# Start of a two-block transformer kernel: raw x transposed by columns, inverse root applied at the first projection's evictions

## The reference

```python
h = rms_norm(x, norm_g[layer])            # x * rsqrt(mean(x*x) + 1e-6) * norm_g
proj = jnp.einsum('bsd,de->bse', h, w_in[layer])   # w_in: 2048 x 8192
qa, ka, va, ga, qb, kb, vb, gb = jnp.split(proj, splits, axis=-1)   # eight of 1024 columns
```

## Time and profile before

| | us |
|---|---|
| three runs: median (lowest to highest) | 1999.19 (1998.39 to 2001.27) |
| the profiled execution, its own time | 2001.09 |
| its span, first to last instruction | 1999.4 |
| TensorE busy | 1921.9 (96% of the span) |
| DVE busy | 1360.1 (68%) |
| ACT busy | 1050.0 (53%) |

### The profile page before, as it was taken

One profiled execution on the slowest core, in us unless ns is written; L12 is line 12 of the kernel. 1 busy time (PEld: TensorE's weight loads), 2 busy tenths in 40 slices (PEclk: granted clock), 3 DMA queues, 4 the chain that ended last, 5 costly groups with the idle time before them and its releaser, 6 DMA issues.

```text
span 1999.4 us, 30270 instructions
## 1 busy us (share of the span) xinstructions
PE 1921.9 (96%) x9674; PEld 1603.0 (80%) x9674; DVE 1360.1 (68%) x1838; ACT 1050.0 (53%) x1687; POOL 104.6 (5%) x181
## 2 busy tenths in 40 slices
PE   7999999999999999999889998999999999999998
PEld 5887887778787777777678777888888888888886
DVE  5677775667777745556777776777777776655555
ACT  5544545554445454446664444556656665544444
POOL 1000001101000013320000000000000000000000
PEclk9999999999999999999999998999999999999999
DMA  7788776578788854336557976577777766555554
GB/s 255 268 292 263 244 260 219 178 244 302 259 290 285 287 167 116 112 125 213 187 194 261 316 248 219 184 244 231 241 230 242 231 220 189 178 186 192 190 192 144
DMA packets 236729, 444.80 MB, mean 222 GB/s; under 512 B 14190, under 2 KB 110027, under 8 KB 235259
## 3 DMA queue, kind: packets, MB, share of 16 engines
q1 hardware_dynamic: 235242, 434.39, 66.0%
q0 software_dynamic: 1424, 9.63, 1.2%
HBM read 439.72 MB, written 4.24 MB: 222 GB/s over the span
## 4 chain that ended last, share of the span: by engine, by line
PE 83%; DVE 6%; ACT 4%; DMA 3%; issue 3%; SPq 1%; DVEq 0%; ACTq 0%
PE PS L1659 51%; PE PS L1969 16%; PE PS L1970 8%; DMA ada_raw<-in_w_ada 3%; PE PS L1690 1%; ACT w_hi L621 1%; DVE arena L1075 1%; PE PS L1748 1%; PE PS L1751 1%; DVE w_lo L1025 1%; PE PS L1734 1%; PE PS L1759 1%; DVE s_sb L1190 1%; PE PS L1688 1%; DVE smx L1198 0%
## 5 line engine op out<-in xcount | busy, mean ns | idle before, releaser
L1025 DVE TENSOR_TENSOR w_lo<-raw,w_hi 128x1024 fp32r<-128x1024 f32 x618 | 755.4, 1224 | 490.3 <-ACT w_hi L621 483.2
L1659 PE MATMUL PS<-w_hi,aT 128*128 128x512 f32 (+1 forms) x3264 | 1049.0, 395 | 16.8 <-ACT arena L757 7.8
L621 ACT ACTIVATE w_hi<-raw 128x1024 fp32r<-128x1024 f32 x618 | 653.6, 1059 | 654.1 <-PE PS L1659 431.9
L1659 PEld LDWEIGHTS PS<-w_hi,aT 128*128 128x128 f32 x3264 | 614.5, 189 | 158.4 <-issue 12.5
L1659 PE MATMUL PS<-w_lo,aT 128*128 128x512 f32 (+1 forms) x1632 | 635.3, 389 | 0.0
L1969 PE MATMUL PS<-aT,w_hi 128*128 128x512 f32 x1408 | 489.3, 394 | 0.3 <-DVE aT L1154 0.3
L1970 PE MATMUL PS<-aT,w_lo 128*128 128x256 f32 x1408 | 390.2, 277 | 0.0
L1659 PEld LDWEIGHTS PS<-w_lo,aT 128*128 128x128 f32 x1632 | 308.6, 189 | 58.8 <-issue 0.2
L1969 PEld LDWEIGHTS PS<-aT,w_hi 128*128 128x128 f32 x1408 | 264.0, 188 | 61.9 <-DVE aT L1154 0.5
L1075 DVE SCALAR_TENSOR_TENSOR arena<-ada_raw,silu_c,arena 128x1024 f32<-128x1024 f32 x192 | 246.5, 1284 | 42.2 <-DMA ada_raw<-in_w_ada 42.1
L1970 PEld LDWEIGHTS PS<-aT,w_lo 128*128 128x128 f32 x1408 | 264.3, 188 | 0.2 <-issue 0.2
(11 more groups left out here) (212 smaller groups left out, 1268.4 us busy)
## 6 DMA issues: line engine op xcount, KB each, us to landing
raw<-in_w_in SPq DMA_DIRECT2D x256, 512.0 KB, 4.1
ada_raw<-in_w_ada SPq DMA_DIRECT2D x192, 512.0 KB, 4.9
raw<-in_w_up SPq DMA_DIRECT2D x176, 512.0 KB, 3.5
raw<-in_w_down SPq DMA_DIRECT2D x88, 512.0 KB, 3.9
raw<-in_w_out SPq DMA_DIRECT2D x32, 512.0 KB, 5.3
raw<-in_w_o SPq DMA_DIRECT2D x32, 512.0 KB, 5.2
raw<-in_w_uq SPq DMA_DIRECT2D x18, 512.0 KB, 5.2
raw<-in_w_ukv SPq DMA_DIRECT2D x16, 512.0 KB, 4.2
```

What stands on the lines that cost most here:

```text
L621: nc.scalar.activation(w_hi[:, m % RING, :], raw[:, m % RING, :], ACT.Copy).then_inc(hi_ready, 1)
L1025: nc.vector.tensor_tensor(w_lo[:, m % RING, :], raw[:, m % RING, :], w_hi[:, m % RING, :].bitcast(F32), ALU.subtract).then_inc(lo_ready, 1)
L1659: mm = pe.matmul(dst, l, r, start=first and j == 0, stop=last and j == 2)
```

## The change

The row factor moves from x to the results, and the start is ordered by what each step needs.

- SP: x comes in three column pieces, 256, 768 and 1024 columns of both tiles, each with its own semaphore and each followed by a weight chunk; chunk 3 follows. The parameters (12 DMAs) come behind the weights. norm_g is loaded by itself, from ACT's queue.
- GpSimd makes `ident` and `zero_c` first and gives `const_ready` 1 for them; the rest is `const_ready` 2.
- TensorE: six transposes of `ident` that nothing reads (`keep_busy`), norm_g's transpose, then the groups of x as plain transposes (raw x, no `diag`), with 6 more idle ones behind group 0 and 12 behind group 3; slot j - 3 follows group j. The six parameter transposes come behind slot 5.
- ACT: norm_g's scale is applied with the column evictions as before; the squares of x come after the splits of slots 6 and 7, silu's Exp and the root behind them.
- DVE: parameter columns in slot 6; mean, silu and the inverse root after slot 7, then the eviction of panel 0.
- Every eviction of the first projection is scaled with the inverse root of its row, a pointer operand: `scaled_out` on DVE (panels 0 to 5, 10, 11), `row_scale` on ACT (6 to 9, and in silu's scale for the gates).
- Panel 0 carries no pieces of w_ada. Row tile 0's four pieces move to slots 1 and 5 of panels 1 and 2, which so carry six each.

```diff
@@ SP @@
-            for s in range(ST):
-                sp.dma_start(X[:, s, :], x[0, s * P:(s + 1) * P, :]).then_inc(x_landed, 16)
-            for j in range(2):
-                load_chunk(W_IN, j, 4 * N_A * HD, first=True)
-            for t, r, src, n in [(0, C_NORM, norm_g, KT), (0, C_PREMIX, g_pre_mix_2, KT),
+            for j, (a, b) in enumerate(X_PIECES):
+                sp.dma_start(X[:, :, a:b], x[0, :, a:b].rearrange("(s p) n -> p s n", p=P)).then_inc(x_landed[j], 16)
+                load_chunk(W_IN, j, C_B0, first=True)
+            load_chunk(W_IN, RING - 1, C_B0, first=True)
+            for t, r, src, n in [(0, C_PREMIX, g_pre_mix_2, KT),
...
-            panels(6, W_IN, C_B0, upto(W_IN, 0), g1_ada(0), free_ada_done=4)
+            panel(W_IN, C_B0, upto(W_IN, C_B0 + PANEL))
+            with T.loop(2, ready_lo_ready=8, free_ada_done=6) as i:
+
+                def two_rows(slot):
+                    g1_ada(1)(i, slot)
+                    if slot in (1, 5):
+                        load_ada(0, i * (2 * 1024) + 1024 * (slot // 4))
+
+                panel(W_IN, i * PANEL + (C_B0 + PANEL),
+                      lambda j: load_chunk(W_IN, j, i * PANEL + (C_B0 + 2 * PANEL)), two_rows)
+            panels(3, W_IN, C_B0 + 3 * PANEL, upto(W_IN, 0), g1_ada(3), free_ada_done=4)
@@ ACT @@
+            act.dma_start(PARAM[C_NORM:C_NORM + KT, 0, :], norm_g.rearrange("a (r n) -> (a r) n", n=P))\
+               .then_inc(norm_landed, 16)
...
-                    nc.scalar.activation(d, PS[:, s, 0:d.shape[-1]], ACT.Copy).then_inc(acc_free[s], 1)
+                    nc.scalar.activation(d, PS[:, s, 0:d.shape[-1]], ACT.Copy,
+                                         scale=row_scale(s) if row_scale else 1.0).then_inc(acc_free[s], 1)
...
+            for slot in range(SLOTS):
+                if slot >= 2:
+                    for j in COLUMNS[slot]:
+                        columns_hi(j, aT_hi, *norm)
+                split()
+                if slot >= 6:
+                    s = slot - 6
+                    for xl in x_landed:
+                        act.wait_ge(xl, 16)
+                    nc.scalar.activation(X_SQ, X[:, s, :], ACT.Square, accum_out=squares[:, s:s + 1])\
+                        .then_inc(act_step, 1)
+                    act.wait_ge(act_step, T.ready(act_step))
             act.nop().then_inc(var_ready, 1)
+            act.wait_ge(par_ready, 2)
+            nc.scalar.activation(silu_c[:], col[:, C_C:C_C + KT], ACT.Exp, scale=-1.0).then_inc(silu_ready, 1)
             root(0)
@@ DVE @@
+            def scaled_out(dst):
+
+                for s in range(ST):
+                    products(s)
+                    nc.vector.tensor_scalar(dst(s), PS[:, s, :], stat[:, 8 + s:9 + s], None, ALU.mult)\
+                        .then_inc(acc_free[s], 1)
...
+            def qkv_b(p, more=None):
+                for slot in range(SLOTS):
+                    g1_slot(slot, p)
+                    if more is not None and slot in (1, 5):
+                        ada(ADA_1, more + slot // 4, 0)
+                scaled_out(lambda s: QKV_B[:, s, ds(p * PANEL, PANEL)])
...
             mean(0, [D])
-            inverse_rms(0)
-            dve.wait_ge(const_ready, 1)
-            diagonals(0)
...
+            inverse_rms(0)
+            scaled_out(lambda s: QKV_B[:, s, 0:PANEL])
@@ TensorE @@
+            def keep_busy(n, bank):
+
+                for _ in range(n):
+                    pe.transpose(PS[:, bank, 0:P], ident[:], ident[:])
...
             pe.wait_ge(const_ready, 1)
-            pe.wait_ge(par_landed, 16 * 13)
...
-            first_panel(lambda s, k: X[:, s, P * k:P * (k + 1)], lambda k: 0)
+            keep_busy(6, B_O)
+            pe.wait_ge(norm_landed, 16)
+            pe.transpose(PS[:, 6, 0:KT], PARAM[0:KT, 0, :], ident[0:KT, 0:KT]).then_inc(norm_T, 1)
+            base = T.ready(aT_ready, 8) - 8
+            for j in range(SLOTS):
+                if j in (0, 1, 4):
+                    pe.wait_ge(x_landed[(0, 1, 4).index(j)], 16)
+                transpose_group(j, lambda s, k: X[:, s, P * k:P * (k + 1)])
+                if j in (0, 3):
+                    keep_busy((6, 12)[j // 3], B_O)
+                if j >= 3:
+                    pe.wait_ge(aT_ready, base + j - 2)
+                    chunk(j - 3, KT)
+            for slot in range(5, SLOTS):
+                pe.wait_ge(aT_ready, base + slot + 1)
+                chunk(slot, KT)
...
+            pe.wait_ge(par_ready, 2)
```

More of the change, by code:

```diff
@@ L756, in gate @@
                     products(s)
[L757 removed]
+                    nc.scalar.activation(gates[:, s, :], PS[:, s, :], func,
+                                         scale=row_scale(s) if row_scale else 1.0).then_inc(acc_free[s], 1)
             SP_ = ACT_PANEL
[L761 to L763 removed]
+            norm = (lambda k: col[:, C_NORM + k:C_NORM + k + 1], lambda k: zero_c[:])
+            act.wait_ge(const_ready, 1)
+            act.wait_ge(par_ready, 1)
+            for j in range(AHEAD):
+                columns_hi(j, aT_hi, *norm)
+                split()
+            columns_hi(3, aT_hi, *norm)
+            for slot in range(SLOTS):
+                if slot >= 2:
+                    for j in COLUMNS[slot]:
+                        columns_hi(j, aT_hi, *norm)
+                split()
+                if slot >= 6:
[5 more added lines that the diff above has]
+                    act.wait_ge(act_step, T.ready(act_step))
             act.nop().then_inc(var_ready, 1)
+            act.wait_ge(par_ready, 2)
+            nc.scalar.activation(silu_c[:], col[:, C_C:C_C + KT], ACT.Exp, scale=-1.0).then_inc(silu_ready, 1)
             root(0)
[L766 to L771 removed]
             squares_b(0)
@@ L821, in panel @@
                     if slot == SLOTS - 1 and func is not None:
-                        gate(func, gates)
+                        gate(func, gates, inv_x if func == ACT.Silu else None)
                         if func == ACT.Silu:
@@ L1072, in ada @@
                 dve.wait_ge(ada_landed[j], T.ready(ada_landed[j], 16))
[L1073 removed]
+                part = acc[:, ds(half * 1024, 1024)]
                 dve.wait_ge(ada_done, T.ready(ada_done, 0))
@@ new lines, in _ @@
+            norm = lambda k: col[:, C_NORM + k:C_NORM + k + 1]
+            for j in range(AHEAD):
+                columns_lo(j, aT_lo, aT_hi, norm)
+                split()
+            columns_lo(3, aT_lo, aT_hi, norm)
+            for slot in range(SLOTS):
+                if slot >= 2:
+                    for j in COLUMNS[slot]:
+                        columns_lo(j, aT_lo, aT_hi, norm)
+                split()
+                if slot == 6:
+                    dve.wait_ge(const_ready, 2)
+                    dve.wait_ge(par_T, 1)
+                    for t, r in enumerate(PARAM_ROWS):
+                        r0 = 0 if t else KT
+                        last = nc.vector.tensor_copy(col[:, P * t + r0:P * t + r],
+                                                     PS[:, 6 + t // 4, P * (t % 4) + r0:P * (t % 4) + r])
+                    last.then_inc(par_ready, 1)
@@ L1300, in _ @@
+            with T.loop(2, **G1) as i:
+                qkv_b(i + 3)
             dve.wait_ge(sums_b_ready, 1)
```

90 lines of the change are left out of this document (41 added, 49 removed).

## The result

20 runs of each kernel: the changed one takes 2003.69 us in the median (1997.59 to 2014.62), the one before 1999.33; the ratio is 1.0024 with a 95% interval of 1.0014 to 1.0034. It is **slower by 0.24%**, some 4.4 us from the medians, where 1995.8 (range 1991.5 to 2001.5) had been forecast. The profiled execution took 2003.98 us, its span is 2002.0, against 2001.09 and 1999.4 before: 2.6 more in the spans.

What follows compares the result with a forecast made beforehand. TensorE, busy 96% of the span, was taken as the bound, waiting longest at the start. 8.65 - 3.2 - 0.6 - 1.5 = 3.35 us gained, from median 1999.19 to 1995.8, range 1991.5 to 2001.5.

Steps and rivals of the forecast that it cites:

- The start: Before and through panel 0: first product at 12.3 us, panel 1 at 39.7 instead of 48.35, 8.65 us gained.
- I take 7.2: At the start: x's second piece lands at 7.2 us, bounds 6.9 and 7.6, from 1.57 MB at 395 GB/s.
- The new wait: Border of panels 0 and 1: DVE's eviction waits for the late inverse root; panel 1 starts 3.1 us after the bias matmul.
- What would show it: Listed signs: first product near 12.3, panel 1 near 39.7 after DVE's eviction, panels 1 and 2 of 23.5 and 24.6 us.
- Panels 1 and 2: Six w_ada pieces instead of four: panels of 23.5 and 24.6 us, 3.2 us lost, bounds 0.5 and 12.6.
- 15.3 + two landings: Panel 2's two-buffer w_ada load chain ends 15.3 us in plus landings of 5.6 and 3.7, giving 24.6 us.
- TensorE's clock: Half rate after new stalls: 0.2 us lost after the first border, 1.3 behind panel 2, 1.5 in all.
- Evictions with a pointer: First projection's 128x512 evictions with a pointer scale take 0.76 us; 0.6 us lost in all, upper bound 5.6.
- (c): Rival: landings bind panels 1 and 2, 12.6 us lost at 7.0 each, 2005.2; loss once their mean passes 5.5; chance 0.12.
- (b): Rival: the added loads in panels 1 and 2 are hidden, costing 0.5, and no clock falls; 1991.6 us, chance 0.20.
- (d): Rival: the pointer's cost grows in proportion to eviction size; 2002.6 us, chance 0.06.
- (a): Rival: idle transposes bring full clock before x's second piece, so 24 passes take 2.6 us, not 5.1; 1993.3, chance 0.12.

Runs made afterwards that it cites:

- e12_after_again: The changed kernel measured once more, unchanged, on the same chip as the run before it: 2004.01 us, ratio 1.0022 to the kernel before.
- e4_before6: The kernel before with only the w_ada loads changed, none in panel 0 and six in panels 1 and 2: 2006.88 us, ratio 1.0036.
- e1_move10: The changed kernel with row tile 0's four w_ada pieces moved from panels 1 and 2 to 10 and 11: 1998.48 us, ratio 0.9990 to before.
- e2_early: The changed kernel with squares in slots 4 and 5, root in slot 6, silu behind the first eviction: 2001.72 us, ratio 1.0008 to before.
- e6_add_only: The changed kernel without the four extra w_ada loads of panels 1 and 2, DVE still doing their multiply-adds on on-chip data: 2002.44 us, ratio 1.0003.
- e3_both: The changed kernel with row tile 0's w_ada loads in panels 10 and 11 and squares and root early: 1994.61 us, ratio 0.9975 to before.
- e5_load_only: The changed kernel with the four extra w_ada pieces loaded and waited for, DVE taking only a 128x16 corner of each: 2004.80 us, ratio 1.0024.
- e9_two_pieces: e3_both with x in two pieces of 1024 columns, two weight chunks behind each, no idle transposes: 1994.30 us, ratio 0.9963 to before.
- e8_x_first: e3_both with x in pieces of 256, 256, 512 and 1024 columns, first w_in chunk behind the third: 1997.22 us, ratio 0.9975 to before.

## Why the prediction was wrong

By its own steps, against the profiled execution:

- **The start: mis-sized by 1.5.** 8.65 forecast, 7.18 measured. The failed step is "I take 7.2" for x's second piece, with 7.6 as its upper bound: it landed at 9.50, 7.67 behind its issue. 395 GB/s was taken from 8 KB rows of two transfers of 1 MB. Two things were wrong in it, by the trace's packets. The rate was lower: the 1.57 MB that were to be through at 7.2 were moved at 7.59. The rest, 1.9 us, is that a piece lands with its last packet. Half of its 256 packets had ended at 6.22 and the last at 9.17, while 0.7 MB of later transfers (chunk 1, the third piece) went by. The prediction let the bytes pass strictly in order, so that the piece had all of the bandwidth until it was complete. In the repetition (e12_after_again) the two times are 7.40 and 9.10. The first product lost only 1.5 of these 2.3, since the 24 passes behind the landing took 4.3 us and not 5.1; the 12 idle ones took 0.15 each in the mean, for the clock rose to full at 13.2.
- **The new wait: right.** 2.88 against 3.1 from the bias matmul to panel 1, ended by DVE's eviction, as listed under "What would show it".
- **Panels 1 and 2: 6.7 lost, not 3.2. This step decided the sign.** Its form was right: "15.3 + two landings". In panel 2 it reads 15.7 + 6.04 + 4.28 = 26.05 (the second load was issued 1.57 behind the first's landing, and 3.2 passed from the second's landing to the next panel's product). In panel 1: 14.5 + 7.12 + 4.00 = 25.65. The landings in the chain average 5.4, where 4.65 was taken, the mean of 5.6 and 3.7. One of the two is long and one short, as the prediction had it, but both were priced too low. That price is the step that failed: 2.8 of the 3.5 us missed. The 3.7 is a chunk of w_in behind a quiet spell, not a piece of w_ada. No piece of w_ada issued in these two panels of the kernel before landed in less than 4.46 us. The issues views give the median landing, first of the kernel before (48 to 93 us), then of the changed one (41 to 93):

```profile
ada_raw<-in_w_ada SPq DMA_DIRECT2D x8, 512.0 KB, 5.7
```

```profile
ada_raw<-in_w_ada SPq DMA_DIRECT2D x12, 512.0 KB, 5.5
```

So the added loads did not make the landings of w_ada longer. They were as long before, but with four pieces a panel hardly any wait of DVE hung on them (2.0 us in these two panels, 4.5 in the changed kernel), and with six, two stand in series. e4_before6 puts 6.8 on this part alone, e1_move10 and e2_early show that it is not the root. The DVE work that came with the loads was mis-sized too: 0.5 was taken for it alone, and e6_add_only has 3.1, half clock included.

- **TensorE's clock: 2.7, not 1.3, behind panel 2.** The earlier trace rows show 3.3 us at half; the changed kernel got 6.8 us twice (in its repetition, 3.4 after each of panels 1 and 2, and none at the first border). That the first border's is mostly hidden, because panel 1 waits for DVE anyway, was right for this kernel: e2_early has no half clock there and takes 25.07, 0.6 less. It holds only with six pieces in panel 1: without them it costs 1.5 (23.93 against 22.43, e1_move10 against e3_both).
- **Evictions with a pointer: right.** 128x512 took 0.76 in the chain and 0.742 in the mean, where 0.76 was taken. The DVE groups of the changed kernel by shape:

```profile
L1099 DVE TENSOR_SCALAR arena<-PS,stat 128x512 f32 x12 | 8.4, 742 | 0.0
```

The sum, then: 7.18 - 6.73 - 2.71, less 0.23 in panels 4 and 5, is -2.5 where +3.35 stood. Of the difference of 5.8, 1.5 is the landing of x, 3.5 the two panels and 1.2 the clock; the pointers give 0.4 back. The medians lie 4.4 apart where the profiled executions lie 2.9: that rest is spread from run to run (17 us between the extremes of the changed kernel, 6 before), which no profile here explains.

Of the rivals, (c) was the one that happened, at 2004: it had its mechanism, its place and the point from which it decides, a mean landing of 5.5. The measured mean in the chain, 5.4, lies just below; the start and the clock did the rest. Its chance of 0.12 was too low. The trace of before had the deciding number, a median of 5.7 and a mean of 5.5 for w_ada's landings in these very panels, and it was weighed by three single landings instead. And no case put such landings together with a late x and a longer half clock. (b), that the loads are hidden, falls with e5_load_only. (d) falls with the 742 ns. (a), that the idle transposes raise the clock before x's second piece, was true and useless: it was full from 6.4 at the latest, TensorE then waited 2.95 us for x, and it was at half again from 9.8. By the Trainium skill, "TensorE: Matmul & The Clock Gate" (What's actually happening), half rate is the default and activity releases it; the windows agree with that, and show that what is released can be lost again before it is used.

The Trainium skill, "DMA: Bandwidth & Descriptors" (Bandwidth), gives 341 GB/s for a transfer of 1 MB, issued from GpSimd there. By an estimate from that figure x's piece would have come 0.6 later than taken, at 7.8; it landed 2.3 later. The page pointed the right way: the 4.00:6.00 window above (326 GB/s) stands near its 341, and the bytes were moved at 7.59. No rate gives the wait for the last packets.

What stays open: why the first microseconds are slow (see below), which of landings and DVE's work is the larger part, and how much of DVE's lateness a third buffer for w_ada would take away. That wasn't tried.

## What to carry to other kernels

Moved loads are not free because they were free where they came from: ask whether the engine that consumes them has slack in its new place. Here panels 1 and 2 have none (their splits start 6 us late, behind the squares), and panels 10 and 11 take the same loads for 0 to 1.9 us. When a chain contains landings, price them by the same transfer in the same stretch, all of its landings and not a few, and ask how many will stand in series. A piece of a load lands with its last packet, here 1.9 us after its bytes could have been through, for later transfers already use the bandwidth. And put the step that a new wait hangs on (squares, root) two slots before it is needed, as the early version does: a stall costs its own length and often a stretch of half clock behind it.

## What the runs showed of the hardware

- **The first columns of x come slowly at each row length tried.** By the trace's packets, means over each microsecond, e9_two_pieces took 194 to 227 ns for one of 4 KB until 7 us, and 159 for its second megabyte, cut the same way; e8_x_first took 105 to 128 for one of 2 KB in 5 to 8 us and 84 to 88 later; in the changed kernel one of 3 KB took 150 to 166. It is a part of the packets that is slow: the medians are 159, 84 and 121 ns in nearly every one of these microseconds, and in e9_two_pieces 15 to 30% took over 1.3 times as long. The kernel before moved its 8 KB rows at 395 GB/s in the same microseconds, with one transfer for each row tile. What makes the difference was not settled.
- **The length of a half-clock stretch varies for the same stall.** 2.06 us idle before panel 1 was followed by 6.8 us at half in the changed kernel, by 3.4 in e1_move10 and e5_load_only, and by none in e6_add_only and e12_after_again; 4.00 was followed by 6.8, 4.67 by 3.4, and 3.06 (e4_before6, before panel 3) by none. A forecast can put bounds on this term, not a value.
